# Scores of the second network as three fp32r products of high and low parts, and the first tile's two attentions in one task

## The chip, the cores and the metric

The kernel runs on one core of a Trainium2 chip. The metric is the device time of one execution in microseconds (us), the median of several. TensorE (PE in the profile, PEld for its weight loads) multiplies matrices into eight PSUM banks; VectorE (DVE) and ScalarE (ACT) read the banks and work on SBUF; GpSimd (POOL) does little here; SyncE (SP) issues the loads of the weights. Each engine takes its instructions in the order in which the program gives them and waits on semaphores.

## The reference, cut to what matters

Two networks of two layers each run one after the other on 256 rows of 1024. The change touches only the sparse attention of the second network, once in each of its two layers. For each of 8 heads (2 key groups of 4 heads) and each block of 128 queries it is

```python
q = proj[..., q columns] * 64 ** -0.5
o_cmp = softmax over 15 compressed keys            # "compressed"
o_s   = softmax(q @ k_slc.T, causal) @ v_slc       # all blocks are selected: 256 keys
o_w   = softmax(q @ k_win.T, causal) @ v_win       # the window covers all 256 keys
o = g[..., 0] * o_cmp + g[..., 1] * o_s + g[..., 2] * o_w
```

Queries of the first 128 rows (tile i = 0) see 128 keys, those of the second (i = 1) see 256.

## The kernel before, in words

**One plan, five engines.** `script` writes one list of steps; each engine's function runs over that list and issues its own part of each step, so the order of the list is the order on every engine. `P.PB` is a ring of the eight PSUM banks, `ER` and `ET` are rings of SBUF tiles for the scores and their transposes.

**Linear work.** Every weight matrix is split into a high part in fp32r (ACT, `high`) and a low part (DVE, `low`), and each product is three fp32r matmuls (`mm3`, `mm3_onto`, lines 217 to 226). A unit of 2048 weights per partition is used in four parts of 12 matmuls with 256 columns (`t_part`, `kv_values`) or 6 with 512 (`n_part`). `high` of the next unit is listed after a unit's second part, the two halves of `low` after its third and fourth.

**Weaving.** `mix(a, b, share)` lists linear parts from `a` and small steps from `b`; each yields a cost. After a linear part of cost `PART` = 1.44, steps of `b` follow until their sum reaches 1.04 times that of the linear parts. In `second`, `a` is `lin_v`, `lin_q(1)`, `lin_conv`, `lin_conv2`, `lin_out` (24 parts) and `b` is `nsa()`, which takes turns between the attention tasks (`slots`) and a side chain: what is left of the compression and the gating network, then `compressed(0)` and `compressed(1)`.

**A task.** There are 8: two pairs of heads `jp`, two tiles `i`, two attentions `bno`. Each lists `score_pair` (PE: fp32 matmuls of 64 rows, the two key groups alternating between rows 0 to 63 and 64 to 127, line 1621; then a bf16 causal mask added by a matmul of 128 rows, line 1626; `soft`: DVE maximum, line 2138, ACT exponentials, line 1875), `scale` (DVE, lines 2166 to 2175), `weigh` (PE transposes, line 1510, copied out by ACT, line 1883) and `values_t` (line 1655). `slots` with the order (-1, 0, -2, -1) lists in turn n: `scale` of task n-1, scores of task n, values of task n-2, `weigh` of task n-1. Tasks of the second pair of heads wait in the plan for `at.until("q")`, which `lin_q(1)` marks after its last part.

**Compressed steps.** `cmp_scores`, `cmp_max`, `cmp_exp`, `cmp_mask`, `cmp_turn` (transpose, line 1768), `cmp_values` (line 1777), each resting on the one before.

The projections of q and k leave PSUM by one ACT copy (line 1828). The functions are printed below.

Of the kernel before, what the change touches and what calls it, by code (L numbers as in the profile page):

```python
# [8 lines left out]
F = mybir.dt.float32  # L9
R = mybir.dt.float32r  # L10
# [17 lines left out]
PART = 1.44  # L28
NRAW = 3
# [421 lines left out]
def script(P):  # L451
# [6 lines left out]
    identb, chunkb, causalb = m["maskb"][:, 0, :], m["maskb"][:, 1, :], m["maskb"][:, 2, :]  # L458
# [267 lines left out]
    def score_pair(q, k, js, i, bias, mask, rs, q_events):  # L726

        bs, ers = [PB.take() for _ in range(2)], [ER.take() for _ in range(2)]
        K = 128 * (i + 1)
        if i:  # L730
            dense(bs)
        add("score_pair", bs, [[q[64 * hh:64 * hh + 64, j, i * 128:(i + 1) * 128] for hh in range(2)] for j in js],
            [[k(hh, j)[:, 0:K] for hh in range(2)] for j in js], mask, i, q_events)
        for hh in range(2):
            if bias is not None:
                add("biased", bs[hh], 2, K, bias(hh, js, K), ers[hh], P.small(2), rs[hh])
            else:
                add("soft", bs[hh], 2, K, P.small(2), ers[hh], rs[hh])
        PB.give(*bs)
        return ers  # L740
# [349 lines left out]
    def second(l, o, nxt):  # L1090
        cols, pet = o["cols"], o["pet"]
        cols_event = ("cols",) + o["tag"]
        Q, KS, VS, sg, ka = m["q1"], m["k1"], m["vs"], m["sg"], m["ka"]
# [155 lines left out]
        def nsa():  # L1249
            obs, sums, split = {}, [0, 0], []  # L1250

            def part(i, kind, *args):

                if not sums[i]:
                    obs[i], = dense([PB.take()])
                ob = obs[i]
                add(kind, ob, *args[:2], sums[i] == 0, sums[i] == 4, *args[2:])
                sums[i] += 1
                if sums[i] == 5:
                    split.append(i)  # L1260

            def full():
                for i in split:
                    add("o_split", obs[i], range(4), (), (), [O1[:, z, 4:8, i * 128:(i + 1) * 128] for z in (0, 1)], [o1_before], [("o1 nsa", l, i)], 1.0 / ALPHA)
                    PB.give(obs[i])
                split.clear()

            def compressed(i):
# [4 lines left out]
                yield 0.5  # L1273
# [5 lines left out]
                yield 0.9  # L1279
# [4 lines left out]
                yield 0.3  # L1284
# [4 lines left out]
            def task(i, bno, jp):  # L1289

                js, T = (2 * jp, 2 * jp + 1), i + 1
                rs, rc = P.small(4), P.small(4)

                def K(hh, j):
                    return KS[64 * hh:64 * hh + 64, bno - 1, :]
                if jp:
                    yield from at.until("q")
                ers = score_pair(Q, K, js, i, None, causalb, [[rs[:, 2 * hh + n:2 * hh + n + 1] for n in range(2)] for hh in range(2)],
                                 [("q nsa", l, jp), ("k nsa", l), "masks"])
                yield 1.1 + 0.5 * i  # L1300
                gate = gts[:, 24 * i:24 * i + 24].rearrange("p (g j b) -> p g j b", g=2, j=4)[:, :, 2 * jp:2 * jp + 2, bno]
                add("scale", ers, rs, rc, (("gates", l), gate), 128 * T)
                yield 0
                ets = turned(ers, i)
                yield 0.44 * T
                yield from at.until("v")
                outs = [(hh, lambda ob, hh=hh: ob.ap[64 * hh:64 * hh + 64, jp * 256:(jp + 1) * 256].rearrange("p (n q) -> p n q", n=2),
                         VS[:, mt, (bno - 1) * 128 + hh * 64:(bno - 1) * 128 + (hh + 1) * 64],
                         ets[hh].ap[:, 0:2 * T * 128].rearrange("p (n t q) -> p n t q", n=2, t=T)[:, :, mt, :]) for mt in range(T) for hh in range(2)]
                part(i, "values_t", ets, outs, [("v nsa", l)], [("win read", l)])  # L1310
                ET.give(*ets)
                yield 0.45 * T
            main = slots([task(i, bno, jp) for jp in range(2) for i in range(2) for bno in (1, 2)], (-1, 0, -2, -1))
# [46 lines left out]
        acc, tail = swiglu(l, 2, ("ht read", ("second", l, 1), 10), nxt)  # L1360
# [21 lines left out]
    add("end")  # L1382

# [114 lines left out]
def tensor_engine(e, P, steps, T, s):  # L1498
# [130 lines left out]

    def weigh(tb, blocks, er, er_event, et, flip):  # L1630
# [139 lines left out]
    def cmp_values(ob, l, et, first, last):  # L1770
# [4 lines left out]
        for c in range(2):  # L1775
# [5 lines left out]
                    ln_turn=ln_turn, out_piece=out_piece, ffn_turn=ffn_turn, ffn_down=ffn_down, score_pair=score_pair,  # L1781
# [5 lines left out]
def scalar_engine(e, P, steps, T, s):  # L1787
# [36 lines left out]
    def copy(b, src, dst, scale, before, out):  # L1824
# [3 lines left out]
        e.activation(dst, src, ACT.Copy, scale=scale).then_inc(done.up(b.free, *out), 1)  # L1828

# [131 lines left out]
    run(steps, dict(start=start, lead_high=lead_high, high=high, turn_split=turn_split, o_split=turn_split, turn_copy=turn_copy, copy=copy, silu_gate=silu_gate, ln_split=ln_split,  # L1961
# [45 lines left out]
def vector_engine(e, P, steps, T, s):  # L2007
# [10 lines left out]
    def masks():  # L2018
# [4 lines left out]
        e.tensor_copy(m["maskb"][:, 2, :], C("causal")).then_inc(done.up("masks"), 1)  # L2023
# [122 lines left out]

    def ret_scores(l, h, b, q, k, dh, er):
# [15 lines left out]
    def scale(ers, rs, rc, gate, K):  # L2163
# [3 lines left out]
        if gate is not None:  # L2167
            r = rc.rearrange("p (g n) -> p g n", g=2)
# [4 lines left out]
        for hh, er in enumerate(ers):  # L2173
            ev = er.ap[:, 0:2 * K].rearrange("p (n k) -> p n k", n=2)
            e.tensor_tensor(ev, ev, bc(rc[:, 2 * hh:2 * hh + 2], 2, K), ALU.mult).then_inc(done.up(("scaled", er.n)), 1)  # L2175
# [214 lines left out]
    def cmp_turn(l, i, er, tb, et):  # L2390
# [7 lines left out]
                    ffn_split=ffn_split, soft=soft, biased=biased, weigh=weigh, ret_scores=ret_scores, ret_values=ret_values,  # L2398
# [7 lines left out]
def build(nc, I, out_ap):  # L2406
    with ExitStack() as ctx:
# [17 lines left out]
        qkv, v1 = sb("qkv", [128, 4096])[:], sb("v1", [128, 1024])[:]  # L2425

# [55 lines left out]
```

## Time and profile before

| | us |
|---|---|
| median of 3 runs | 1990.39 (1990.3 to 1990.59) |
| profiled execution, its time | 1990.32 |
| its span, first to last instruction | 1988.5 |
| PE busy | 1972.3 (99%) |
| DVE busy | 1246.6 (63%) |
| ACT busy | 911.0 (46%) |

The granted clock of TensorE is 0.999 of full speed. In the profile a matmul's duration overlaps the next ones, so the cost of a matmul in a stream is read from start to start. The stage that the change touches lies at 1217 to 1285 us in the first layer of the second network and at 1711 to 1779 us in the second layer.

### The profile page before, as it was taken

What the parts mean: (1) busy time and instruction counts of PE and PEld (TensorE: products, weight loads), DVE (VectorE), ACT (ScalarE), POOL (GpSimd) and SP (SyncE); (2) the same over time, 40 slices, a digit from 0 to 9 for tenths busy, and PEclk for the clock granted to TensorE, in tenths of its full rate; (3) what the DMA queues carried; (4) which work ended last, traced back from release to release, by engine and by line L of the source; (5) the groups of instructions that cost most, each with busy time, mean ns of one, the idle gap of its engine ahead of it and who ended that gap; (6) DMA issues with size and microseconds to landing.
All of it is one profiled execution on the core that took longest, in us unless ns stands there. A gap on an engine that the chain in (4) does not pass through costs nothing.

```text
span 1988.5 us, 31860 instructions
## 1 busy us (share of the span) xinstructions
PE 1972.3 (99%) x13856; PEld 1800.0 (91%) x13856; DVE 1246.6 (63%) x1772; ACT 911.0 (46%) x1221; POOL 99.7 (5%) x84
## 2 busy tenths in 40 slices
PE   8999999999999999999999999999999999999998
PEld 7888999999888999999999989799999998979997
DVE  6566666555656766655565567665566556776555
ACT  4445544443445544444444445544444444554442
POOL 0000001000100000100100020010010002001000
PEclk9999999999999999999999999999999999999999
DMA  8544566666544456696666646468657665646663
GB/s 291 178 144 137 181 201 197 202 206 187 180 160 148 148 174 199 196 263 179 183 202 188 189 151 174 111 192 258 191 169 213 189 188 148 177 109 194 188 189 106
DMA packets 421445, 361.85 MB, mean 182 GB/s; under 512 B 29424, under 2 KB 361528, under 8 KB 421304
## 3 DMA queue, kind: packets, MB, share of 16 engines
q1 hardware_dynamic: 421160, 359.74, 59.9%
q8 instruction: 109, 1.79, 0.4%
q14 instruction: 32, 0.26, 0.0%
q10 hardware_dynamic: 144, 0.07, 0.0%
HBM read 358.72 MB, written 1.05 MB: 181 GB/s over the span
## 4 chain that ended last, share of the span: by engine, by line
PE 95%; DVE 4%; ACT 1%; issue 0%; DMA 0%; DVEq 0%
PE ps L217 22%; PE ps L218 22%; PE ps L219 22%; PE ps L224 8%; PE ps L226 8%; PE ps L225 8%; PE ps L1510 2%; PE ps L1621 1%; DVE hl L2029 1%; PE ps L1655 1%; DVE small L2134 0%; PE ps L1626 0%; ACT hl L1805 0%; PE ps L1693 0%; DVE er L2132 0%; DVE er L2175 0%
## 5 line engine op out<-in xcount | busy, mean ns | idle before, releaser
L2029 DVE TENSOR_TENSOR hl<-raw,hl 128x1024 fp32r<-128x1024 f32 (+2 forms) x535 | 722.6, 1384 | 383.6 <-ACT hl L1805 383.1
L217 PE MATMUL ps<-xt,hl 128*128 128x256 f32 (+1 forms) x2672 | 754.2, 282 | 0.0
L218 PE MATMUL ps<-xt,hl 128*128 128x256 f32 (+1 forms) x2672 | 746.2, 279 | 0.0
L219 PE MATMUL ps<-xt,hl 128*128 128x256 f32 (+1 forms) x2672 | 745.7, 279 | 0.0
L1805 ACT ACTIVATE hl<-raw 128x2048 fp32r<-128x2048 f32 (+1 forms) x338 | 613.9, 1824 | 219.3 <-PE ps L226 157.4
L217 PEld LDWEIGHTS ps<-xt,hl 128*128 128x128 f32 (+1 forms) x2672 | 500.9, 187 | 5.4 <-issue 2.3
L218 PEld LDWEIGHTS ps<-xt,hl 128*128 128x128 f32 (+1 forms) x2672 | 501.0, 188 | 3.1
L219 PEld LDWEIGHTS ps<-xt,hl 128*128 128x128 f32 (+1 forms) x2672 | 500.8, 187 | 0.2
L224 PE MATMUL ps<-hl,o 128*128 128x512 f32 x656 | 261.3, 398 | 0.0
L226 PE MATMUL ps<-hl,o 128*128 128x512 f32 x656 | 259.0, 395 | 0.0
L225 PE MATMUL ps<-hl,o 128*128 128x512 f32 x656 | 258.8, 394 | 0.0
L217 PE MATMUL ps<-hl,xt 128*128 128x512 f32 (+1 forms) x576 | 207.0, 359 | 0.4 <-DVE hl L2029 0.4
L219 PE MATMUL ps<-hl,xt 128*128 128x512 f32 (+1 forms) x576 | 202.1, 351 | 0.0
L218 PE MATMUL ps<-hl,xt 128*128 128x512 f32 (+1 forms) x576 | 202.0, 351 | 0.0
L1853 ACT ACTIVATE th<-ps 128x256 f32<-128x256 f32 x132 | 50.7, 384 | 329.1 <-PE ps L219 329.1
L226 PEld LDWEIGHTS ps<-hl,o 128*128 128x128 f32 x656 | 123.5, 188 | 28.8
L224 PEld LDWEIGHTS ps<-hl,o 128*128 128x128 f32 x656 | 123.5, 188 | 27.2 <-issue 1.5
L225 PEld LDWEIGHTS ps<-hl,o 128*128 128x128 f32 x656 | 123.7, 189 | 25.5
L217 PEld LDWEIGHTS ps<-hl,xt 128*128 128x128 f32 x576 | 108.4, 188 | 18.5 <-issue 1.7
L219 PEld LDWEIGHTS ps<-hl,xt 128*128 128x128 f32 x576 | 108.3, 188 | 15.9
L218 PEld LDWEIGHTS ps<-hl,xt 128*128 128x128 f32 x576 | 108.5, 188 | 14.5
L2112 DVE SCALAR_TENSOR_TENSOR tm<-th,ps 128x256 f32<-128x256 f32 x132 | 55.5, 421 | 99.2 <-ACT th L1853 95.2
(197 smaller groups left out, 1576.4 us busy)
## 6 DMA issues: line engine op xcount, KB each, us to landing
raw<-in_w_in SPq DMA_DIRECT2D x83, 1024.0 KB, 5.1
raw<-in_w_ffn_in SPq DMA_DIRECT2D x88, 512.0 KB, 5.3
raw<-in_ffn_gate SPq DMA_DIRECT2D x88, 512.0 KB, 4.0
raw<-in_ffn_up SPq DMA_DIRECT2D x88, 512.0 KB, 5.3
raw<-in_ffn_down SPq DMA_DIRECT2D x44, 1024.0 KB, 5.2
raw<-in_w_ffn_out SPq DMA_DIRECT2D x22, 1024.0 KB, 5.2
raw<-in_w_out SPq DMA_DIRECT2D x24, 512.0 KB, 4.8
raw<-in_w_branch_a SPq DMA_DIRECT2D x8, 1024.0 KB, 5.1
```

The costliest lines, as they stand in the source:

```text
L217: e.matmul(out, l[0], r[0], start=start, stop=False)
L218: e.matmul(out, l[0], r[1], start=False, stop=False)
L219: return e.matmul(out, l[1], r[0], start=False, stop=stop)
L224: e.matmul(out, l[0], r[0], start=False, stop=True, skip_group_check=True)
L225: e.matmul(out, l[0], r[1], start=False, stop=True, skip_group_check=True)
L226: return e.matmul(out, l[1], r[0], start=False, stop=True, skip_group_check=True)
L1510: ins = e.transpose(b.ap[:, k * 128:(k + 1) * 128], x, ident)
L1621: ins = e.matmul(b.ap[:, n * K:(n + 1) * K], qs[n][hh], ks[n][hh], start=n == 0, stop=mask is None and n == 1)
L1805: e.activation(m["hl"][:, k % NHL, 0, c], m["raw"][:, k % NRAW, c], ACT.Copy).then_inc(s.high.up(*([("high", k, h)] if parts == 2 else [(" ...
L1853: e.activation(tha, ga, ACT.Tanh, scale=0.5).then_inc(done.up(th.full), 1)
L2029: e.tensor_tensor(lo[:, c], m["raw"][:, k % NRAW, 0:n][:, c], hi[:, c].bitcast(F), ALU.subtract).then_inc(s.low.up(("low", k), *([("low", ...
L2112: e.scalar_tensor_tensor(tma, tha, 1.0, ga, ALU.add, ALU.mult).then_inc(done.up(th.free), 1)
```

## The change: what it does

- q (twice a layer) and k leave PSUM as a high part in fp32r (ACT) and a low part (DVE): `q_parts`, `k_parts`. The plain copy of q stays, for `cmp_scores`; that of k goes. The parts lie in `o2` and in a part of `o1`.
- Scores are `score_parts`: high by high, high by low, low by high, 12 matmuls of 64 rows and 256 columns in fp32r per task, then two mask matmuls in fp32r (`ai`, `ri`): 512 columns for tile 0, 256 for tile 1.
- Tile 0's two attentions with the same pair of heads become one task: 6 tasks in place of 8, each with 512 score columns per key group, 8 transposes and 4 products with the values.
- Costs in the plan: scores 1.3, weigh 0.88, values 0.9; three steps of `compressed(1)` yield `PART`. `PB.spare` is set to False at the start of `lin_conv2`.

```diff
+SCORES = 1.3
+    def score_parts(qs, ks, i, rs, q_events, read):
+        bs, ers = dense([PB.take() for _ in range(2)]), [ER.take() for _ in range(2)]
+        n = len(rs[0])
+        add("score_parts", bs, qs, ks, i, q_events, read)
+        for hh in range(2):
+            add("soft", bs[hh], n, 512 // n, P.small(n), ers[hh], rs[hh])
...
         def lin_q(u):
...
-            copy_t(P.res, Q, 2 * u, 0.125, before_q, ("q nsa", l, u))
+            b, = P.res
+            add("copy", b, halves(b), Q[:, 2 * u:2 * u + 2, :], 0.125, before_q, [("q nsa", l, u)])
+            add("q_parts", b, Q[:, 2 * u:2 * u + 2, :], [QZ[:, z, 2 * u:2 * u + 2, :] for z in (0, 1)], 0.125, ("ht read", ("second", l, 1), 10),
+                ("q nsa", l, u), ("q parts", l, u))
...
-            copy_t(P.res, KS, 0, 1.0, before_q, ("k nsa", l))
+            add("k_parts", b, [KZ[:, z, :, :] for z in (0, 1)], [o1_before], ("k parts", l))
...
         def lin_conv2():
+            PB.spare = False
...
                 add("cmp_scores", l, i, bs, er, kcs)
                 PB.give(*bs)
-                yield 0.5
+                yield PART if i else 0.5
...
                 add("cmp_mask", l, i, er, rs, gts)
-                yield 0.9
+                yield PART if i else 0.9
...
                 ER.give(er)
-                yield 0.3
+                yield PART if i else 0.3
...
-            def task(i, bno, jp):
+            def task(i, bs, jp):
+                js = (2 * jp, 2 * jp + 1)
+                n = 4 if i == 0 else 2
...
+                ers = score_parts(qs, ks, i, [[rs[:, n * hh + x:n * hh + x + 1] for x in range(n)] for hh in range(2)],
+                                  [("q parts", l, jp), ("k parts", l), "masks"], ("parts read", l))
+                yield SCORES
...
-            main = slots([task(i, bno, jp) for jp in range(2) for i in range(2) for bno in (1, 2)], (-1, 0, -2, -1))
+            main = slots([task(i, bs, jp) for jp in range(2) for i, bs in ((0, (1, 2)), (1, (1,)), (1, (2,)))], (-1, 0, -2, -1))
...
@@ tensor_engine
+    def score_parts(bs, qs, ks, i, events, read):
+        for x in events:
+            e.wait_ge(*T[x])
+        for b in bs:
+            e.wait_ge(*T[b.before])
+        for n in range(2):
+            for zq, zk in ((0, 0), (0, 1), (1, 0)):
+                for hh, b in enumerate(bs):
+                    e.matmul(b.ap[:, n * 256:(n + 1) * 256].rearrange("p (t k) -> p t k", t=2), qs[n][hh][zq], ks[hh][zk],
+                             start=n == zq == zk == 0, stop=False)
+        for b in bs:
+            out = b.ap.rearrange("p (n k) -> p n k", k=128) if i == 0 else b.ap.rearrange("p (n k) -> p n k", n=2)[:, :, 128:256]
+            e.matmul(out, m["ai"], bc(m["ri"], 1, 4 if i == 0 else 2), start=False, stop=True).then_inc(done.up(b.full, read), 1)
...
@@ scalar_engine
+    def q_parts(b, whole, dst, scale, before, whole_event, out):
+        e.wait_ge(*T[b.full])
+        e.wait_ge(*T[before])
+        e.activation(dst[0], halves(b), ACT.Copy, scale=scale).then_inc(done.up(b.free, ("parts high",) + out), 1)
...
@@ vector_engine
+    def q_parts(b, whole, dst, scale, before, whole_event, out):
+        e.wait_ge(*T[whole_event])
+        e.wait_ge(*T[("parts high",) + out])
+        e.tensor_tensor(dst[1], whole, dst[0].bitcast(F), ALU.subtract).then_inc(done.up(out), 1)
```

## Rows read from the trace of the kernel before

**Rows 1.** The page: its first line, and busy time by engine.
```profile
span 1988.5 us, 31860 instructions
...
PE 1972.3 (99%) x13856; PEld 1800.0 (91%) x13856; DVE 1246.6 (63%) x1772; ACT 911.0 (46%) x1221; POOL 99.7 (5%) x84
```

**Rows 2.** By window, first layer: us, busy PE, PEld, DVE, ACT, POOL, clock, DMA.
```profile
1217.40:1284.50 67.10, 65.59 (x519) 54.33 (x518) 49.40 (x115) 37.58 (x102) 0.00 (x0) 1.00 0.38 110
```

**Rows 3.** Timeline of PE (start, us, ...): a tile 1 task, then a linear part.
```profile
1228.03 1.14 PE L1621 MATMUL ps<-k,q 64*128 64x256 f32 x8
1229.10 0.39 PE L1626 MATMUL ps<-maskb 128*128 128x256 bf16 x2
...
1229.45 0.28 PE L218 MATMUL ps<-xt,hl 128*128 128x256 f32 x1
...
1230.62 0.28 PE L219 MATMUL ps<-xt,hl 128*128 128x256 f32 x1
```

**Rows 4.** Timeline of PE: the last `weigh`, among output parts of 512 columns.
```profile
1272.10 0.40 PE L224 MATMUL ps<-hl,o 128*128 128x512 f32 x1
...
1272.57 0.40 PE L226 MATMUL ps<-hl,o 128*128 128x512 f32 x1
1273.69 1.26 PE L1510 MATMUL ps<-cst,er 128*128 128x128 f32 x8 [0.72 <-DVE er L2175]
1274.70 0.48 PE L224 MATMUL ps<-hl,o 128*128 128x512 f32 x1
```

**Rows 5.** Timeline of PE: a tile 0 task between linear parts.
```profile
1221.89 0.28 PE L219 MATMUL ps<-hl,xt 128*128 128x256 f32 x1
1222.10 0.71 PE L1621 MATMUL ps<-k,q 64*128 64x128 f32 x8
1222.75 0.39 PE L1626 MATMUL ps<-maskb 128*128 128x256 bf16 x2
...
1223.10 0.28 PE L218 MATMUL ps<-hl,xt 128*128 128x256 f32 x1
```

**Rows 6.** The page's costliest groups: weight loads of the linear work.
```profile
L217 PEld LDWEIGHTS ps<-xt,hl 128*128 128x128 f32 (+1 forms) x2672 | 500.9, 187 | 5.4 <-issue 2.3
```

**Rows 7.** Timeline of PE: values of a tile 1 and of a tile 0 task.
```profile
1246.38 1.08 PE L1655 MATMUL ps<-et,v 128*64 128x256 f32 x8
...
1261.90 0.65 PE L1655 MATMUL ps<-et,v 128*64 128x256 f32 x4
```

**Rows 8.** Timelines of ACT, DVE and PE where the first scores begin.
```profile
1217.61 0.60 ACT L1828 ACTIVATE q<-ps 128x512 f32<-128x512 f32 x1 [1.90 <-PE ps L219]
...
1218.14 1.22 DVE L2029 TENSOR_TENSOR hl<-raw,hl 128x1024 fp32r<-128x1024 f32 x1
...
1219.51 0.40 DVE L2347 TENSOR_SCALAR sg<-sg,small 128x256 f32<-128x256 f32 x1
...
1219.35 0.71 PE L1621 MATMUL ps<-k,q 64*128 64x128 f32 x8
```

**Rows 9.** Timeline of ACT around the second projection of q.
```profile
1230.72 0.48 ACT L1875 ACTIVATE er<-ps,small 128x256 f32<-128x256 f32 x1 [2.82 <-DVE small L2138]
...
1232.67 1.93 ACT L1805 ACTIVATE hl<-raw 128x2048 fp32r<-128x2048 f32 x1
...
1240.86 0.61 ACT L1828 ACTIVATE q<-ps 128x512 f32<-128x512 f32 x1
...
1241.40 1.12 ACT L1883 ACTIVATE et<-ps 128x512 f32<-128x512 f32 x2
```

**Rows 10.** Timelines of DVE and PE: the end of the second compressed chain.
```profile
1277.40 0.35 DVE L2367 TENSOR_TENSOR er<-ps,cst 128x60 f32<-128x60 f32 x2 [0.57 <-PE ps L1761]
...
1280.72 0.27 DVE L2380 TENSOR_REDUCE small<-er 128x8 f32<-128x120 f32 x1
...
1281.67 0.28 DVE L2388 TENSOR_TENSOR er<-er,small 128x120 f32<-128x120 f32 x1
...
1283.85 1.13 PE L1777 MATMUL ps<-et,gb 120*128 120x256 f32 x4 [0.78 <-DVE et L2393]
```

More of the change, by code:

```diff
@@ L1249, in nsa @@
         def nsa():
-            obs, sums, split = {}, [0, 0], []
+            obs, sums, split = {}, [3, 5], []
+            first = [True, True]
             def part(i, kind, *args):
-                if not sums[i]:
+                if first[i]:
                     obs[i], = dense([PB.take()])
[L1256 to L1259, printed above, removed]
+                sums[i] -= 1
+                add(kind, obs[i], *args[:2], first[i], sums[i] == 0, *args[2:])
+                first[i] = False
+                if sums[i] == 0:
                     split.append(i)
@@ L1263, in full @@
                 for i in split:
-                    add("o_split", obs[i], range(4), (), (), [O1[:, z, 4:8, i * 128:(i + 1) * 128] for z in (0, 1)], [o1_before], [("o1 nsa", l, i)], 1.0 / ALPHA)
+                    add("o_split", obs[i], range(4), (), (), [O1[:, z, 4:8, i * 128:(i + 1) * 128] for z in (0, 1)], [("parts read", l)], [("o1 nsa", l, i)], 1.0 / ALPHA)
                     PB.give(obs[i])
@@ L1287, in compressed @@
                 yield 1.0
-            def task(i, bno, jp):
[L1291 to L1295, printed above, removed]
+            def task(i, bs, jp):
+                js = (2 * jp, 2 * jp + 1)
+                n = 4 if i == 0 else 2
+                rs, rc = P.small(2 * n), P.small(2 * n)
                 if jp:
                     yield from at.until("q")
[L1298 to L1302, printed above, removed]
+                qs = [[[QZ[64 * hh:64 * hh + 64, z, j, i * 128:(i + 1) * 128] for z in (0, 1)] for hh in range(2)] for j in js]
+                ks = [[KZ[64 * hh:64 * hh + 64, z, 0:2, 0:128] if i == 0 else KZ[64 * hh:64 * hh + 64, z, bs[0] - 1, :].rearrange("p (t k) -> p t k", t=2)
+                       for z in (0, 1)] for hh in range(2)]
+                ers = score_parts(qs, ks, i, [[rs[:, n * hh + x:n * hh + x + 1] for x in range(n)] for hh in range(2)],
+                                  [("q parts", l, jp), ("k parts", l), "masks"], ("parts read", l))
+                yield SCORES
+                gate = gts[:, 24 * i:24 * i + 24].rearrange("p (g j b) -> p g j b", g=2, j=4)[:, :, 2 * jp:2 * jp + 2, :]
+                add("scale", ers, rs, rc, (("gates", l), gate[:, :, :, 1:3] if i == 0 else gate[:, :, :, bs[0]]), 512 // n)
@@ L1359, in second @@
         layer_norm(acc, out_end(I["w_out_2"][l], acc, [[("o1 nsa", l, i)] for i in range(2)], P.o1_read, heads=True))
-        acc, tail = swiglu(l, 2, ("ht read", ("second", l, 1), 10), nxt)
+        acc, tail = swiglu(l, 2, ("parts read", l), nxt)
         layer_norm(acc, tail, final=l == DEPTH - 1)
@@ L1382, in script, with halves @@
     add("end")
+def halves(b):
+    return b.ap.rearrange("p (c t) -> p c t", c=2)
 def quarter(banks, c):
@@ L1828, in copy, with k_parts @@
         e.activation(dst, src, ACT.Copy, scale=scale).then_inc(done.up(b.free, *out), 1)
+    def q_parts(b, whole, dst, scale, before, whole_event, out):
+        e.wait_ge(*T[b.full])
+        e.wait_ge(*T[before])
+        e.activation(dst[0], halves(b), ACT.Copy, scale=scale).then_inc(done.up(b.free, ("parts high",) + out), 1)
+    def k_parts(b, dst, before, out):
+        e.wait_ge(*T[b.full])
+        for x in before:
+            e.wait_ge(*T[x])
+        e.activation(dst[0], halves(b), ACT.Copy).then_inc(done.up(("parts high",) + out), 1)
     def silu_gate(l, b, th, tm, dst, before, out):
@@ L1959, in cmp_exp @@
         e.activation(er.ap[:, 0:120], er.ap[:, 0:120], ACT.Exp).then_inc(done.up(("cmp exp", l, i)), 1)
-    run(steps, dict(start=start, lead_high=lead_high, high=high, turn_split=turn_split, o_split=turn_split, turn_copy=turn_copy, copy=copy, silu_gate=silu_gate, ln_split=ln_split,
+    run(steps, dict(start=start, lead_high=lead_high, high=high, turn_split=turn_split, o_split=turn_split, turn_copy=turn_copy, copy=copy, q_parts=q_parts, k_parts=k_parts, silu_gate=silu_gate, ln_split=ln_split,
                     seed=seed, ffn_gate=ffn_gate, ffn_turn=ffn_turn, ffn_split=ffn_split, soft=soft, biased=biased,
@@ L2022, in masks @@
         e.tensor_copy(m["maskb"][:, 1, :], C("chunk")).then_inc(done.up(), 1)
-        e.tensor_copy(m["maskb"][:, 2, :], C("causal")).then_inc(done.up("masks"), 1)
+        e.tensor_copy(m["ai"][:, :], C("causal")).then_inc(done.up(), 1)
+        e.tensor_copy(m["ri"][:, :], C("ident")).then_inc(done.up("masks"), 1)
     def low(k, n, h, parts):
@@ L2145, in weigh, with k_parts @@
             e.tensor_copy(et.ap[:, 0:w], tb.ap[:, 0:w]).then_inc(done.up(et.full, tb.free), 1)
+    def q_parts(b, whole, dst, scale, before, whole_event, out):
+        e.wait_ge(*T[whole_event])
+        e.wait_ge(*T[("parts high",) + out])
+        e.tensor_tensor(dst[1], whole, dst[0].bitcast(F), ALU.subtract).then_inc(done.up(out), 1)
+    def k_parts(b, dst, before, out):
+        e.wait_ge(*T[("parts high",) + out])
+        e.tensor_tensor(dst[1], halves(b), dst[0].bitcast(F), ALU.subtract).then_inc(done.up(out, b.free), 1)
     def ret_scores(l, h, b, q, k, dh, er):
```

33 lines of the change are left out of this document (21 added, 12 removed).

## Prediction

> **What bounds the kernel now.** I read the page first: TensorE is busy 99% of a span of 1988.5 us, DVE 63% and ACT 46% [rows 1]. So the time is the sum of what PE issues, plus the few places where it stands still, and the change can act in two ways only: by the matmuls that it adds or removes, and by waits that it removes or makes. Then the attention stage alone, by window: 67.1 us, of which PE is busy 65.6, DVE 49.4 and ACT 37.6 [rows 2]. DVE has three quarters of the stage filled, and it works in order, so a result that PE needs soon can be late there although no engine but PE is full. The same stage stands once more in the second layer, so I work out one and double it. Last I went through the timeline of PE in the stage, looking at each step from the linear matmul ahead of it to the linear matmul behind.
>
> **Scores on PE.** Linear matmuls of 256 columns follow each other by 0.117 us (ten steps from 1229.45 to 1230.62 [rows 3]); those of 512 columns by 0.235 (1272.10 to 1272.57 in two steps [rows 4]). A tile 0 task takes 1223.10 - 1221.89 less two such steps, 0.98 us; 0.09 of it is the way in (1221.89 to 1222.10 less 0.117) and 0.65 the eight score matmuls [rows 5]. For tile 1 the eight take 1.07, and the task 1.42 - 0.117 + 0.09 = 1.39 [rows 3]. Eight matmuls of twice the columns cost 0.42 more: if the two key groups run side by side, four pairs cost 0.105 for each 128 columns and 0.23 is fixed. After the change a task is six pairs of 256 columns. No fp32r matmul of 64 rows stands in the trace; the bounds are a pair at 0.117, side by side as the fp32 ones are, and 0.234, one behind the other. The shape with two groups of rows is that of L1621, the data type that of the linear work, and both rows point to 0.117; I take it. Tile 1: 0.09 + 0.23 + 6 x 0.117 + 2 masks x 0.117 = 1.25, tile 0 with masks of 512 columns 1.49. The masks were bf16; in fp32r their weight load is that of L217, 0.187 [rows 6], and may show by 0.1 a task. Per layer 4 x (1.39 - 1.25) + 2 x (2 x 0.98 - 1.49) = 1.5, or 0.9 with the load. For the values, two blocks of 0.65 become one of 1.08 [rows 7]: 0.22, twice a layer. The transposes stay 48. Both layers: 2.7 to 3.9 us less; I take 3.3.
>
> Each score matmul has its own load of 0.187 [rows 6], and the linear matmuls, each with such a load, still start every 0.117 [rows 3]: the load is hidden there behind a matmul on the same rows. The Trainium skill says otherwise ("TensorE: Matmul & The Clock Gate", Part 3, what overlaps): a weight load overlaps a running matmul only if their row groups differ. By that rule the second pair would wait for its load, and the scores would get dearer in place of cheaper; the row speaks against it for this form, and the rule is weighed as a rival below. The fixed 0.23 and the 0.09 sit where the form changes between 128 and 64 rows [rows 5]; six tasks pay them in place of eight, which is in the sum.
>
> **The parts of q, first pair of heads.** Scores now wait for `q_parts`: ACT copies q, ACT writes the high part, DVE subtracts. The last part of `lin_q(0)` ends, ACT copies from 1217.61 for 0.60, and PE begins the first scores at 1219.35, one linear part later [rows 8]. The high part would be done near 1218.8. But DVE runs a `low` half from 1218.14 to 1219.36, then the gates' small step; the subtraction takes the place of the L2347 that starts at 1219.51. Half a `low` half is 0.61, so with a PSUM source some 0.65: the low part is there at 1220.2, and PE stands about 0.9 us. The floor, with DVE free, is 0.1; nothing in the change moves that `low` half, so I take 0.9. Behind the waiting scores stands all of PE: no linear part can pass.
>
> **The parts of q, second pair.** I walked the plan's two accounts (linear parts of 1.44 times 1.04 against the new costs). The tasks in the new order are A (tile 0), B and C (tile 1), then D, E, F for the second pair. D's turn comes right behind the last part of `lin_q(1)`, with only the two transposes of `turn_split` between (sums 11.56 against 11.98, so this is no close call). Before, the first task that needed this q came three linear parts later. The floor of the wait: copy 0.6, high part 0.6, low part 0.65, less the transposes: 1.6. And ACT is behind: from C's maximum it has four exponentials (1.9), a `high` (1.93), a tanh (0.26), a turn copy (0.4, taken between the small and the large copies), two copies of transposes (1.12), the q copy and the high part (0.61 each) [rows 9], 6.8, then DVE 0.65: 7.5. PE from the end of C's scores to D has three linear parts of 1.40, values 1.08 and twelve transposes of some 0.11: 6.6. C's maximum lies 0.7 to 1.6 behind its scores (half of a `scale` and a reduce may be ahead). So PE stands 1.6 to 2.6 us; I take 2.2. The k parts come early (a linear unit and `lin_q(0)` lie between) and cost nothing but 0.65 of DVE.
>
> **The last `weigh`.** Before, PE stood there: 1272.57 to 1273.69 in place of 0.235, 0.9 us, and the eight transposes took 1.01 [rows 4]. DVE was the late one: its queue held both convolution taps and two `low` halves ahead of that `scale`. In the new order the `scale` of F is listed behind the second part of `lin_conv2`, ahead of both taps, and F's scores three linear parts earlier; the wait goes: 0.9 a layer, 1.8 in all (0 to 2.2).
>
> **The compressed steps.** Before, PE stood 0.78 us ahead of the last `cmp_values` [rows 10]. With the new costs `cmp_max` follows `cmp_scores` at once (1.44 is less than 1.44 x 1.04), `cmp_turn` comes two output parts (2 x 1.41) behind `cmp_scores`, `cmp_values` one further. The chain on DVE needs 0.35, the maximum and subtraction 0.6, a `low` half that is listed between 1.22, and the mask steps 1280.72 to 1281.95, 1.23 [rows 10]: 3.4 against 2.8, so PE now stands 0.6 at `cmp_turn`; then a `low` half and the product, 1.9, against a part of 1.41: 0.4 more. One wait of 0.78 becomes two of 1.0 together: +0.4 for both layers (-1.6 to +1.0).
>
> **Sum.** The profiled execution took 1990.32, its span 1988.5, the 1.8 around it do not change; the median is 0.07 above it. 1990.3 - 3.3 (PE) - 1.8 (weigh) + 1.8 (first q parts) + 4.4 (second) + 0.4 (compressed) = 1991.8. What the change saves on PE it gives back in two new waits. `PB.spare` earlier, the later event of `o_split` and the two mask copies I cost at nothing: the banks that they name are free a linear part before, the copies run in a stage where DVE has gaps. With all terms at their low ends the sum is 1990.3 - 3.9 - 2.2 + 0.2 + 3.2 - 1.6 = 1986.0, at their high ends 1990.3 - 2.7 + 2.0 + 5.2 + 1.0 = 1995.8.
>
> **Rivals.**
> *The pairs do not run side by side.* Each of the 12 tasks pays 6 x 0.117 = 0.70 more, 8.4 in all: 2000. A second way to the same end: each pair stands until its load of 0.187 [rows 6] is in, 1.1 a task, 13.5 in all: 2005. For both: no row of this form. Against them: the fp32 pairs [rows 3, 5]. They decide from 0.04 us more a pair, 72 pairs. The rule of the Trainium skill ("TensorE: Matmul & The Clock Gate", Part 3) would bring the second way; no run here shows it yet.
> *The q parts are in time.* If ACT and DVE are ahead of PE where I have them behind, both waits go: 1985.2. For it: ACT is busy only 37.6 of 67.1 us [rows 2]. Against it: the floor of 1.6 at D is made of three operations in series. It decides where the two waits of a layer sum to less than 0.3.
> *DVE stays late to the end.* The subtractions add 2 us a layer to a queue that is three quarters full; the wait at the last `weigh` stays (+1.8), D waits 2.6 (+0.8), the compressed steps stand at their high end (+0.6): 1995. For it: the queue that was back to back ahead of 1273 [rows 4]. Against it: fewer reduces, and the taps now come behind.
>
> **How the numbers follow.** Two runs of this kernel can be told apart from about 0.2%, 4 us. My forecast, 0.60: 1991.8, inside it. Pairs not side by side, or waiting for loads, 0.12: 2000 to 2005. Parts in time 0.12: 1985.2. DVE late 0.16: 1995. Faster is the second rival, 0.12; slower the first and third, 0.28; the same 0.60. The range leaves out the first rival and the lower edge of the second: 1985.5 to 1997; the forecast's own is 1988.5 to 1994.3.
>
> **What the profile after would show.** Pairs of `score_parts` 0.117 apart, a task of tile 1 near 1.25; PE idle ahead of the scores of A by 0.9 and of D by about 2.2, released by DVE at the subtraction of `q_parts`; no idle time at the last `weigh`; two short waits at the end, ahead of `cmp_turn` and of `cmp_values`. Wrong would make me: pairs 0.234 apart, no idle time ahead of D, or a wait in tasks B, C, E, F that I have not listed, from the eight exponentials of A and D, which hold DVE in `scale`.

## The result and the profile after

The median is 1996.02 us (7 runs, 1994.6 to 1998.0), against 1990.59 of the kernel before, run beside it (7 runs, 1990.16 to 1991.51): a ratio of 1.0028 with an interval of 1.0018 to 1.0037. The change makes the kernel slower by 0.3%, 5.4 us. That lies in the range of the prediction (1985.5 to 1997), but 4.2 us above its figure, above the forecast's own 1988.5 to 1994.3, and on the side to which it gave 0.28. The profiled execution took 1998.0, the upper end of the runs.

The page of the kernel after, first line and busy time:

```profile
span 1996.2 us, 31855 instructions
...
PE 1974.2 (99%) x13864; PEld 1804.7 (90%) x13864; DVE 1247.4 (62%) x1755; ACT 912.2 (46%) x1217; POOL 98.7 (5%) x84
```

The waits of PE in the kernel after (us in total, times, longest), without those that stood before as well:

```profile
PE ps L1662 <- DVE o L2200: 5.6, 4, 2.1
...
PE ps L1534 <- DVE er L2235: 1.5, 2, 0.7
PE ps L1815 <- DVE et L2453: 1.0, 2, 0.5
...
PE ps L1806 <- DVE er L2448: 0.7, 2, 0.4
```

These are four places in each layer: the scores of A and D behind the subtraction of `q_parts` (L1662 behind L2200), the last `weigh` behind the `scale` of F (L1534 behind L2235), `cmp_values` of tile 0 (L1815) and `cmp_turn` of tile 1 (L1806). The first and the last were forecast; the second should have gone; the third was not listed.

The timeline of PE in the kernel after, first layer, in order: A; a task of tile 1 and the first two linear matmuls behind it; D and the linear matmuls behind it; `cmp_values` of tile 0; the last `weigh`; the end of the second compressed chain:

```profile
1220.82 0.97 PE L1662 MATMUL ps<-o 64*128 64x256 f32 x12 [0.70 <-DVE o L2200]
1221.72 0.73 PE L1666 MATMUL ps<-ri,ai 128*128 128x512 f32 x2
...
1224.17 0.97 PE L1662 MATMUL ps<-o 64*128 64x256 f32 x12
1225.07 0.51 PE L1666 MATMUL ps<-ri,ai 128*128 128x256 f32 x2
1225.41 0.28 PE L218 MATMUL ps<-hl,xt 128*128 128x256 f32 x1
1225.53 0.28 PE L219 MATMUL ps<-hl,xt 128*128 128x256 f32 x1
...
1240.17 0.38 PE L1534 MATMUL ps<-cst,sg 128*128 128x128 f32 x2
1242.63 1.65 PE L1662 MATMUL ps<-o 64*128 64x256 f32 x12 [2.08 <-DVE o L2200]
1244.21 1.22 PE L1666 MATMUL ps<-ri,ai 128*128 128x512 f32 x2
1245.23 0.41 PE L218 MATMUL ps<-xt,hl 128*128 128x256 f32 x1
1245.44 0.41 PE L219 MATMUL ps<-xt,hl 128*128 128x256 f32 x1
...
1246.20 0.28 PE L220 MATMUL ps<-xt,hl 128*128 128x256 f32 x1
1246.32 0.28 PE L218 MATMUL ps<-xt,hl 128*128 128x256 f32 x1
...
1267.03 1.13 PE L1815 MATMUL ps<-et,gb 120*128 120x256 f32 x4 [0.52 <-DVE et L2453]
...
1275.21 1.25 PE L1534 MATMUL ps<-cst,er 128*128 128x128 f32 x8 [0.73 <-DVE er L2235]
...
1286.34 0.33 PE L1806 MATMUL ps<-cst,er 128*120 128x128 f32 x1 [0.36 <-DVE er L2448]
...
1288.07 1.13 PE L1815 MATMUL ps<-et,gb 120*128 120x256 f32 x4
```

The same twelve score matmuls take 0.90 us up to the masks in A and in the task of tile 1 (1221.72 less 1220.82), and 1.58 in D; and the linear matmuls behind D start every 0.21 us, not every 0.117 [rows 3], until 1246.2. Work that is the same takes twice as long: the reader should look at the clock.

Windows of the kernel after around D, first and second layer (us, busy PE, PEld, DVE, ACT, POOL, granted clock, DMA share, GB/s):

```profile
1240.10:1242.50 2.40, 0.45 (x4) 0.21 (x3) 2.40 (x5) 1.37 (x4) 0.00 (x0) 1.00 0.00 0
1242.50:1246.30 3.80, 3.67 (x20) 3.25 (x21) 3.22 (x8) 0.53 (x3) 0.00 (x0) 0.55 0.76 255
...
1738.50:1740.90 2.40, 0.45 (x6) 0.45 (x8) 2.37 (x6) 1.07 (x3) 0.00 (x0) 1.00 0.01 3
1740.90:1744.70 3.80, 3.80 (x23) 3.38 (x20) 2.70 (x5) 1.54 (x9) 0.00 (x0) 0.55 0.80 280
```

In both layers PE was busy for 0.45 of 2.4 us, and then the granted clock was 0.55 for 3.8 us: most of that stretch at the lower level, 1.2 GHz. Before [rows 2] it stood at 1.00 in this stage. So D costs more than the time in which PE stands ahead of it.

Timelines of DVE, then of ACT, in the kernel after: the subtraction for A, that for D, the product for `cmp_values` of tile 0 (L2453), and the instructions ahead of the `scale` of F:

```profile
1218.84 1.22 DVE L2079 TENSOR_TENSOR hl<-raw,hl 128x1024 fp32r<-128x1024 f32 x1
...
1220.09 0.68 DVE L2200 TENSOR_TENSOR o<-q,o 128x512 fp32r<-128x512 f32 x1
...
1240.76 1.22 DVE L2079 TENSOR_TENSOR hl<-raw,hl 128x1024 fp32r<-128x1024 f32 x1
1241.89 0.69 DVE L2200 TENSOR_TENSOR o<-q,o 128x512 fp32r<-128x512 f32 x1
...
1266.30 0.68 DVE L2453 TENSOR_TENSOR et<-ps,cst 120x512 f32<-120x512 f32 x1
...
1268.03 0.68 DVE L2365 TENSOR_TENSOR zb<-th,ps 128x512 f32<-128x512 f32 x1
1273.44 0.69 DVE L2091 SCALAR_TENSOR_TENSOR o<-ps,o 128x512 fp32r<-128x512 f32 x1 [4.74 <-ACT o L1853]
1274.05 0.17 DVE L2225 RECIPROCAL small<-small 128x4 f32<-128x4 f32 x1
```

```profile
1240.37 0.60 ACT L1866 ACTIVATE q<-ps 128x512 f32<-128x512 f32 x1 [0.26 <-PE ps L220]
1240.86 0.59 ACT L1871 ACTIVATE o<-ps 128x512 fp32r<-128x512 f32 x1
...
1271.01 1.91 ACT L1843 ACTIVATE hl<-raw 128x2048 fp32r<-128x2048 f32 x1
1272.81 0.60 ACT L1853 ACTIVATE o<-ps 128x512 fp32r<-128x512 f32 x1
```

Both subtractions (L2200) stand behind a `low` half (L2079), that of A with one step of 0.20 between. Ahead of F's `scale` (L2225) DVE is not full, it stands idle for 4.74 us: it waits for the first half of `o_split`, which ACT (L1853) does only behind a `high` of 1.91 (L1843). The matching row of before is in [rows 4]; the same 0.7 us of wait had another cause there.

### The profile page after: what moved, and what is told of

Same layout as the page of the kernel before. It is cut to its first block, busy times and chain, and to the rows that moved or that the text cites. A ratio compares the mean times of both kernels' runs of the same rounds, so it can differ in the third digit from the quotient of the medians.

```text
span 1996.2 us, 31855 instructions
## 1 busy us (share of the span) xinstructions
PE 1974.2 (99%) x13864; PEld 1804.7 (90%) x13864; DVE 1247.4 (62%) x1755; ACT 912.2 (46%) x1217; POOL 98.7 (5%) x84
## 4 chain that ended last, share of the span: by engine, by line
PE 91%; DVE 5%; ACT 2%; issue 1%; DMA 0%; DVEq 0%
PE ps L218 21%; PE ps L219 21%; PE ps L220 21%; PE ps L225 8%; PE ps L227 8%; PE ps L226 8%; PE ps L1534 2%; DVE hl L2079 1%; ACT hl L1843 1%; DVE er L2235 1%; PE ps L1693 1%; ACT er L1924 0%; PE ps L1645 0%; DVE small L2184 0%; DVE small L2188 0%
## 5 line engine op out<-in xcount | busy, mean ns | idle before, releaser
L2079 DVE TENSOR_TENSOR hl<-raw,hl 128x1024 fp32r<-128x1024 f32 (+2 forms) x535 | 722.8, 1384 | 388.3 <-ACT hl L1843 387.7
L1843 ACT ACTIVATE hl<-raw 128x2048 fp32r<-128x2048 f32 (+1 forms) x338 | 613.8, 1824 | 219.3 <-PE ps L227 160.8
```

The lines of the kernel that those rows point to most:

```text
L1843: e.activation(m["hl"][:, k % NHL, 0, c], m["raw"][:, k % NRAW, c], ACT.Copy).then_inc(s.high.up(*([("high", k, h)] if parts == 2 else [(" ...
L2079: e.tensor_tensor(lo[:, c], m["raw"][:, k % NRAW, 0:n][:, c], hi[:, c].bitcast(F), ALU.subtract).then_inc(s.low.up(("low", k), *([("low", ...
```

## The experiments

The reasons to be told apart: (1) waits for the parts of q, (2) the clock that falls behind the wait of D, (3) the order around `o_split`, (4) the matmuls themselves, (5) the spacing of the compressed steps. The first kernel has matmuls that serve nothing, and one takes its scores as plain fp32 products; the others are the changed kernel with steps or matmuls in another order.

**D's wait filled with matmuls.** Nine matmuls of 512 columns, whose result is overwritten, are issued ahead of D's wait for the parts.

```diff
     def score_parts(bs, qs, ks, i, events, read):
-        for x in events:
-            e.wait_ge(*T[x])
         for b in bs:
             e.wait_ge(*T[b.before])
+        if i == 0 and events[0][2]:
+            for _ in range(9):
+                e.matmul(halves(bs[0]), XT[:, 0, 0, 0:128], XT[:, 0, 0:2, :], start=True, stop=True)
+        for x in events:
+            e.wait_ge(*T[x])
```

> The changed kernel, with nine fp32r matmuls of 512 columns put ahead of the wait of task D in each layer (2.1 us of work in a bank that the scores then overwrite; the outputs stay). Theory, the clock: the scores of D cannot begin sooner, DVE's subtraction still releases them, but TensorE does not stand still and the granted clock stays at its upper level; in the changed kernel it lay at the lower one for 3.4 us after each of the two waits, which costs 1.7 us each. So 3.4 us less than the profiled execution of the changed kernel (1998.0) and some 2 to 3 less than its median (1996.0): 1993 to 1994.5, the runs closer together. Rival, the slow stretch has nothing to do with the idle time (the transfers or the banks make it): the clock row stays at 0.55 after D, and the time is 1996 or more.

1994.58 (10 runs, 1994.33 to 1995.22), ratio 1.0021 (1.0011 to 1.0031), 0.1 above the expected range. A window of this kernel over D's scores and what follows:

```profile
1242.00:1246.00 4.00, 4.00 (x37) 3.61 (x38) 3.28 (x8) 1.50 (x9) 0.00 (x0) 1.00 0.78 262
```

D starts as late behind the transposes as without the fill (1241.96 less 1239.49, 2.47 us), the clock stays at 1.00, and the median is 1.4 lower. The runs lie within 0.9 us instead of 3.4. So the fall of the clock is 1.4 us of the median, and it is what spreads the runs.

**D two linear parts later.** The plan lets D in behind the second part of `lin_conv`.

```diff
             PB.give(b)
-            if u:
-                at.mark("q")
             yield PART
...
         def lin_conv():
-            yield from t_parts(*t_proj(w_in, 0))
+            for n, cost in enumerate(t_parts(*t_proj(w_in, 0))):
+                yield cost
+                if n == 0:
+                    at.mark("q")
```

> The changed kernel, with the tasks of the second pair of heads let in one linear part of lin_conv later, so that task D follows two linear parts (2.8 us) after the second projection of q. Theory, the wait at D and the clock that falls with it cost 2.1 + 1.7 us a layer: D does not wait, the clock stays up, 7.6 us less than the profiled 1998.0, 1988.5 to 1991 with what the later steps lose at the end of the stage (the last scale then stands behind a convolution tap). Rival, DVE is late everywhere and the wait only moves: idle time of 2 us a layer turns up in tasks D, E or F or at the compressed steps, and the time stays above 1994.

1990.20 (10 runs, 1989.89 to 1990.89), ratio 0.9998 (0.9989 to 1.0008): 5.8 us less than with the change as it was. D no longer waits, and the clock stays up. `compressed(0)` waits in the plan for the same mark, so it moves too, and the waits at the last `weigh`, at `cmp_values` and at `cmp_turn` (3.2 in all) are gone as well: the 5.8 is not D's alone. The new waits of PE in this kernel, in E and F, where the rival had put them, and what is left at A:

```profile
PE ps L1535 <- ACT et L1933: 4.1, 4, 1.4
PE ps L1663 <- DVE o L2201: 1.4, 2, 0.7
```

L1535 is `weigh`, L1933 the ACT copy behind it. The two results of one task's transposes took the same PSUM bank, one after the other, so the second waited for the copy of the first. In the plan this comes from `PB.spare = False`, which now leaves one bank of the right kind for both: the list that `script` writes for this kernel gives one bank to both results of E and to both of F (bank 2 in the first layer, bank 1 in the second), where that of the changed kernel gives two.

**The ready halves read after the side step.** `o_split` of tile 0 is then listed one linear part behind `cmp_values` and ahead of the `weigh` of E; in the changed kernel it comes two parts behind, after that `weigh` and a `high`.

```diff
-                ready = list(split)
                 x = next(side, IDLE)
+                ready = list(split)
```

> The changed kernel, with the o_split of tile 0 listed one linear part earlier, right behind the compressed values that complete its sum, ahead of the weigh of task E. Theory: the last weigh waits because DVE stood 4.7 us at that o_split, whose ACT part was listed behind a high copy of 1.9 us, with the scale of F behind it; ahead of them the idle 0.7 us at the last weigh goes in both layers, 1.5 to 1.8 us less than the changed kernel, 1994.3. Rival, the queue of DVE as a whole is the cause (the taps, the low halves): the wait at the last weigh stays within 0.2 us of 0.7.

1993.62 (10 runs, 1992.13 to 1995.59), ratio 1.0015 (1.0005 to 1.0024): 2.4 less. The wait at the last `weigh` is gone from the list; those at A, D, `cmp_values` and `cmp_turn` stand as they were. From the linear matmul ahead of the last `weigh` to the one behind it there are now 0.91 us (1271.93 to 1272.84), in the changed kernel 2.02 (1274.20 to 1276.22): 1.1 a layer, 2.2 of the 2.4, more than the idle time that the list of waits gives (0.73 a layer). So the order of `o_split` alone held F's `scale`. The profiled execution of this kernel gave something more, in the timeline of PE at D and in the windows ahead of and behind D's start:

```profile
1241.89 0.97 PE L1662 MATMUL ps<-o 64*128 64x256 f32 x12 [2.08 <-DVE o L2200]
1242.79 0.73 PE L1666 MATMUL ps<-ri,ai 128*128 128x512 f32 x2
1243.36 0.28 PE L218 MATMUL ps<-xt,hl 128*128 128x256 f32 x1
1243.48 0.28 PE L219 MATMUL ps<-xt,hl 128*128 128x256 f32 x1
```

```profile
1239.30:1241.80 2.50, 0.51 (x5) 0.27 (x3) 2.50 (x5) 1.43 (x4) 0.00 (x0) 1.00 0.00 0
1241.80:1245.50 3.70, 3.61 (x33) 3.23 (x34) 3.11 (x8) 1.08 (x7) 0.00 (x0) 1.00 0.81 262
```

The same wait of 2.08, and the clock stays at 1.00. So the fall does not come in every execution. The fall's price can be read from the two kernels: from D's first score to the linear work 1.47 here (1241.89 to 1243.36) against 2.60 with the clock down (1242.63 to 1245.23), and some four linear steps at 0.21 in place of 0.117: 1.13 + 0.4, about 1.5 us each time it happens.

**The merged task with plain fp32 scores.** Scores as before the change (four fp32 pairs of 256 columns a task), no parts of q and k; everything else as changed.

```diff
-            for zq, zk in ((0, 0), (0, 1), (1, 0)):
+            for zq, zk in ((0, 0),):
...
-                                  [("q parts", l, jp), ("k parts", l), "masks"], ("parts read", l))
+                                  [("q nsa", l, jp), ("k nsa", l), "masks"], ("parts read", l))
```

> The changed kernel without the high and low parts: scores as plain fp32 matmuls of 64 rows and 256 columns (4 a task in place of 12), k copied as before, no q_parts and k_parts; tile 0's two attentions in one task, fp32r masks and the spaced steps stay. Theory: the waits of A and D are those of the parts; here A waits for nothing and D for one copy (about 0.5), the clock does not fall; scores cost 1.63 (tile 0) and 1.39 (tile 1) a task plus 0.1 for the masks' loads. By the sum 1990.3 - 1.5 (PE) + 1.0 (D) + 1.0 (the compressed values of tile 0) = 1990 to 1991.5. Rival, the merged tasks and the order make the loss: above 1994 with idle time at D of more than 1.5.

1991.93 (10 runs, 1991.14 to 1992.64), ratio 1.0006 (0.9997 to 1.0016), 0.4 above what was expected. These runs have 1.8 to 3.0 us of their time outside the span from first to last instruction, every other kernel here 1.8; the median span is 1989.4, which with 1.8 would lie in the expected range. A does not wait, D 0.45 for the plain copy; the waits at F, `cmp_values` and `cmp_turn` stand. The parts of q thus lose 4.1 us net in this order (4.8 by the spans, 1994.2 against 1989.4): what the fp32r matmuls save is less than what they wait and what the clock costs behind D.

**Score matmuls one key group behind the other.**

```diff
-        for n in range(2):
-            for zq, zk in ((0, 0), (0, 1), (1, 0)):
-                for hh, b in enumerate(bs):
+        for hh, b in enumerate(bs):
+            for n in range(2):
+                for zq, zk in ((0, 0), (0, 1), (1, 0)):
```

> The score matmuls of a task in the order of the key group, all six of one group ahead of the six of the other, in place of pairs. The arithmetic is the same. Theory (pairs run side by side, each pair 0.117): twelve matmuls of 64 rows behind each other take 0.117 each, 0.70 more a task, 12 tasks: +8.4, so 2002 to 2006, and blocks of tile 1 near 2.04 in place of 1.336. Rival (a pair is not side by side, or waits for its loads, so that the order is of no weight): no change, 1994 to 1998, blocks of 1.336.

1997.54 (4 runs, 1997.33 to 2000.32), ratio 1.0038 (1.0025 to 1.0052). The time lies below the theory's 2002 and in the range of the rival; the blocks decide, and they agree with neither. The timeline of PE, the same task of tile 1 as above:

```profile
1224.01 1.32 PE L1662 MATMUL ps<-o 64*128 64x256 f32 x12
1225.26 0.51 PE L1666 MATMUL ps<-ri,ai 128*128 128x256 f32 x2
```

From first score to mask 1.25 in place of 0.90: 0.35 a task, half of the 0.70 expected. So pairs do run side by side, and the order matters; but of the six steps that the order should have added only three (3 x 0.117) came. The single records of such a block show how: matmuls start at 0, 0.22 and 0.34 us, then one at 0.35 that lasts 0.38, as only the first matmul of each group does in the paired order (the others last 0.28), and the rest up to 1.04, some two at a time. So the second group began 0.35 after the first, ahead of the first group's last three: against what the start of this document says of every engine, TensorE did not start these matmuls strictly in the order of the program. For 12 tasks 0.35 is 4.2 us; 1994.58 (the change with the clock held up, as it was behind D in the profiled execution here) and 4.2 make 1998.8. In this run D waits 1.75 in place of 2.08 and `cmp_values` 0.2 in place of 0.5, which takes off 1.3: 1997.5, the measured time.

**The spacing undone.** The three yields of the compressed steps as before; a single execution first, then timed.

```diff
-                yield PART if i else 0.5
+                yield 0.5
...
-                yield PART if i else 0.9
+                yield 0.9
...
-                yield PART if i else 0.3
+                yield 0.3
```

> The changed kernel with the costs of the compressed steps of tile 1 as in the kernel before (the spacing undone); the order of all other steps stays. Theory (spacing moves one wait into two of about the same sum): TensorE stands 0.7 to 0.9 ahead of the last cmp_values of a layer in place of 0.35 and 0.17 ahead of cmp_turn and cmp_values, the span is 0.3 to 0.8 longer for both layers together, other waits as they were. Rival (the spacing is a loss of its own): the span is 1 us or more shorter, with less than 0.3 of waits at the end of a layer's attention.

2003.29 in one execution, outside what either expectation gave. TensorE stood 1.77 at `cmp_turn` and 0.78 at `cmp_values` of tile 1, and the clock fell behind them. So it was run again with timing:

> The spacing of the compressed steps undone, once more and timed: one execution gave 2003.3 us, with TensorE standing 1.8 at cmp_turn and 0.8 at cmp_values of tile 1 in each layer and the granted clock at its lower level behind them. Theory: without the spacing 2.0 us a layer are lost to these waits against the changed kernel, and the clock falls there in part of the executions: median 1999 to 2003. Rival (that execution was an odd one): 1995.5 to 1997.5, as the changed kernel.

2003.89 (4 runs, 2003.2 to 2004.98), ratio 1.0068 (1.0054 to 1.0081), 0.9 above the theory and far from the rival. The waits of PE at the two lines (`cmp_values` of both tiles), and the windows at the end of the attention of the first and the second layer:

```profile
PE ps L1806 <- DVE er L2448: 3.5, 2, 1.8
PE ps L1815 <- DVE et L2453: 2.6, 4, 0.8
```

```profile
1284.00:1288.50 4.50, 3.54 (x10) 2.74 (x11) 1.76 (x4) 0.60 (x1) 0.00 (x0) 0.70 0.00 0
...
1782.80:1790.00 7.20, 4.66 (x15) 3.33 (x14) 4.58 (x11) 2.15 (x5) 0.00 (x0) 0.83 0.35 91
```

Without the spacing the changed kernel would lose 7.9 us more. The waits at the end grow from 0.53 a layer to 2.55, 4.0 in all, and the clock falls there in both layers (0.70 and 0.83 over the windows) as it did behind D. Behind D itself it fell in this execution in the second layer alone (0.79 over 1740 to 1748 us; 1.00 over 1239 to 1249 in the first), after waits of 2.06 and 2.07; the single execution before shows the same. That makes three falls, against two in the profiled execution of the changed kernel; these two executions differ by 5.2 (2003.2 against 1998.0), near the 4.0 of the waits and one fall of about 1.5. The rest of the 7.9 was not broken down. The spacing pays, but against a loss that the rest of the new order makes.

**Three orders together.** D late, `o_split` right behind `cmp_values`, and `PB.spare = False` no longer set at the start of `lin_conv2` (it is set there three parts in, by `take_acc`, as before the change).

```diff
         def lin_conv2():
-            PB.spare = False
             for n, cost in enumerate(t_parts(*t_proj(w_in, 256))):
```

> Three edits of the changed kernel together: D let in two linear parts later, the list of ready halves read after the side step, and the bank rule PB.spare back where the kernel before had it. In the run with D late alone, TensorE stood 4.1 us in all at the weigh of E and F, released by the ACT copy of the weigh before: with the rule set early both results of a weigh take the same bank one after the other. Theory: with the rule late they have two banks again, and the order of o_split keeps scale F in time, so these 4.1 us go and nothing takes their place; 1990.2 less 3 to 4.1 gives 1986 to 1987.5, faster than the kernel before, with the only listed waits of the attention stage those of A (1.4 in all). Rival (the banks only show a late DVE or ACT): the weigh of E or F waits as long for something else; 1989.5 to 1991.

1988.60 (11 runs, 1988.31 to 1989.26), ratio 0.9990 (0.9981 to 0.9999). The 4.1 us behind the ACT copies are gone, but the last `weigh` now waits 1.3 a layer behind its `scale`, so the gain is 1.6: between the two expectations. The list of steps gives two banks again (2 and 5 to the results of E, 3 and 2 to those of F in the first layer). The two edits that came on top of D late were not run one by one. It is the first version ahead of the kernel before.

**And A one linear part later.**

```diff
                     if i == 0 or k0 == 0:
                         yield PART
+                    at.mark("v1")
...
-                if jp:
-                    yield from at.until("q")
+                yield from at.until("q" if jp else "v1")
```

> The run before, and the scores of A one linear part of the values projection later. Theory: the subtraction of the first q parts is then done (it ends 0.7 us into that linear part), the 1.4 us of A go too and the span falls by 1.0 to 1.4 below the run before: 1984.8 to 1986.5. Rival: A's later scores push B, C and the exponentials behind them, and the wait comes back there or at D: the same as the run before, within 0.5.

1987.03 (11 runs, 1986.72 to 1987.39), ratio 0.9982 (0.9973 to 0.9991): 3.5 us faster than the kernel before and 9 faster than the change as it was, the latter by the order of the steps and the banks alone. The gain of 1.6 over the run before is what the theory said, a little more than its 1.0 to 1.4; the time is 0.5 above its range, which had been reckoned from a faster run before. The waits of PE in this kernel, complete but for the start of the kernel:

```profile
PE ps L1534 <- DVE er L2235: 2.6, 2, 1.3
PE ps L1693 <- DVE small L2225: 1.0, 2, 0.5
PE ps L218 <- DVE hl L2079: 0.4, 1, 0.4
```

No score, no compressed step waits any more. The last two rows stood in the kernel before as well.

**The taps one side step later**, behind the `scale` of F (one more `yield` ahead of `conv_taps`).

> The fastest kernel so far (D late, ready halves after the side step, banks as before, A one part later) and the two convolution taps one side step later, behind the scale of F. Theory: the 1.3 us that TensorE stands in each layer at the weigh of F are DVE's first tap ahead of that scale (1.35 us in two instructions); with the tap behind it the wait goes, 2.6 in all, but the compressed steps of tile 1 come one linear part later and lose part of their spacing, so 0.5 to 1.5 us come back: 1985.3 to 1986.6. Rival (DVE has no slack left behind F): all of it comes back as waits at cmp_turn and cmp_values, 1986.7 to 1988.

1988.44 (11 runs, 1987.97 to 1989.08), ratio 0.9989 (0.9980 to 0.9998), above both expectations and 1.4 slower than without this edit. It all comes back, as the rival said, but mostly by another wait than it named: the wait at `weigh` is gone, but the output work now stands 1.6 a layer for `conv_split`, the end of the convolution that the taps feed (3.1 in all), and `cmp_turn` 0.4. On DVE the `scale` of F and the taps are both needed in time, and either order makes PE wait for the other.

## Why the prediction was near in time and wrong in kind

By its own steps, for both layers:

- **Scores and values on PE: -3.3 forecast, about -2.9 measured.** A task of tile 1 takes, in the way of [rows 3], 1225.53 - 1224.17 - 0.117 + 0.09 = 1.33 (forecast 1.25, and 1.35 if the masks' load shows; it shows). A task of tile 0 takes 1243.48 - 1241.89 - 0.117 + 0.09 = 1.56 where the clock held (forecast 1.49). Four times 1.39 - 1.33, twice 2 x 0.98 - 1.56, and the 0.44 of the values, taken as forecast, are 1.5 a layer. The steps of 0.117 stand: six pairs and the fixed 0.23 take 0.90 (forecast 0.93). The first rival is excluded by these rows. The Trainium skill ("TensorE: Matmul & The Clock Gate", Part 3) says that a weight load overlaps a running matmul only where their row groups differ. This trace does not agree with it for this form: each of the twelve matmuls has its own load of 0.184, and the pairs, which use the same two groups of rows each time, still follow each other by 0.117.
- **First parts of q: +1.8 forecast, 1.5 measured** (1220.82 follows the linear matmul ahead by 0.98; 0.117 of it is that matmul's step and 0.09 the way in, which the task above already has), for the reason given: a `low` half, then the gates' step, then the subtraction.
- **Second parts of q: +4.4 forecast, 4.2 to 4.3 measured** (2.08 idle; 2.46 from the transposes at 1240.17 to the scores, less their 0.2 and the way in). The size was right and one half of the working was not: ACT was not behind. Its copy of q starts as soon as PE ends the projection (1240.37, idle 0.26 ahead). What was added to the floor of 1.6 is the `low` half at 1240.76 on DVE.
- **The last `weigh`: -1.8 forecast, 0 measured. This step failed.** The step took DVE's queue ahead of the `scale` of F to hold the taps and `low` halves alone, and of `o_split` the prediction named only a later event, at no cost. But the sum of tile 0 is now completed by `cmp_values`, listed behind D's values (before, the values of the second pair of heads came behind it); its `o_split` is listed two linear parts later, and ACT does it behind a `high` of 1.91. The `scale` of F is listed early, as the step said, but behind a DVE instruction that waits 4.74. The run with the ready halves read later removes the wait, which is worth 2.2 us, and shows that nothing else holds it. It is the result of the third rival (the wait stays) without its mechanism (a full DVE).
- **`cmp_values` of tile 0: not in the sum, +1.0.** It is listed right behind D's values; its `cmp_turn` is on PE at 1263.82, but DVE does the `scale` of E and the maxima of F first, then its product (L2453, at 1266.30).
- **Compressed end: +0.4 forecast, about -0.5 measured** (0.36 at `cmp_turn` and 0.40 - 0.235 at `cmp_values`, against 0.78 [rows 10]), within the bounds. The step was held against the kernel before; what the spacing does within the new order, 7.9 us, it did not ask.
- **The clock: not in the sum, +1.4 in the median.** The prediction priced D's wait by its length. In the profiled execution, where it fell in both layers, it cost about 3 (twice 1.5).

From the 1990.6 of the kernel before (its 7 runs beside the result) the measured terms make 1990.6 - 2.9 + 1.5 + 4.3 + 1.0 - 0.5 = 1994.0, where the kernel with the clock held up took 1994.58; 0.6 is not placed. The clock's 1.4 is the difference of that run to the 1996.0 of the result. The forecast of no measurable change failed by the two steps that were not in the sum and the one that was wrong, 1.8 + 1.0 + 1.4 = 4.2, all of one sign; that what the other terms were off by cancels, the 0.6 among it, is luck.

Open: why the clock falls behind D's wait in some executions and holds in others. The runs of the changed kernel, 1994.6 to 1998.0, would fit none, one or two falls of some 1.5, but only the profiled executions show how many there were. The mean granted clock that is on record for each run mostly goes along: with the ready halves read later it is 0.999 in the three runs at 1992.1 to 1992.3, 0.998 in the four at 1993.5 to 1993.8 and 0.997 in the two at 1995.3 and 1995.6, but 0.999 in the one at 1994.4.

Not run: plain fp32 scores in the last, fastest order, and the kernel before with its steps moved in this way. So how much of the 3.5 us over the kernel before is owed to the fp32r scores, and how much to the merged tasks and the order, is open.

## What to carry to other kernels

A new operation between a producer and the engine that sets the time can cost its latency, not its duration (here TensorE stood 0.7 us at A and 2.1 at D for a subtraction of 0.68 and what was ahead of it): place its consumer one or two units of work later in the plan before judging the operation. Here the same instructions in another order went from 0.3% slower to 0.2% faster. A wait of TensorE is to be priced with what the clock may do after it, and an order of steps that a planner works out is to be printed: the forecast, which walked it, missed two of the four places of waiting.

## What the runs showed of the hardware that was not expected

- After TensorE had been busy 0.45 of 2.4 us, the granted clock was 0.55 for the next 3.8 us in both layers of one execution, and 1.00 behind the same wait in an execution of another kernel with the same D. In two executions without the spacing it stayed at 1.00 behind D in the first layer and fell in the second. With the wait filled by matmuls it stayed at 1.00 in both layers of the profiled execution.
- fp32r matmuls of 64 rows and 256 columns on the two halves of the rows run in pairs 0.117 us apart, the step of one fp32r matmul of 128 rows. With one half's six issued all behind the other's they still overlapped in part: the second half's first started 0.35 us after the first half's, beside three that stood ahead of it in the program, and a task took 0.35 us more, not 0.70.
